# Input projection: history and edges in one piece, second weights split before the root, 1104 columns instead of 1152, odd squares...

## The reference, cut to what matters

```python
u = rmsnorm(h, norm_mix)          # h: (1088 + 16 rows, 1024)
p = u @ w_in                      # to 3336 columns
# SSD group: xbc = silu(causal_conv(p[conv columns], buf, conv_w, conv_b)), dt = softplus(p[dt] + dt_bias), z = p[gate]
# RWKV group: prev = concat([shift_buf, p[:, :-1]]); pm = p + (prev - p) * shift_mu
```

## Time and profile before

| | us |
|---|---|
| median of 3 runs | 4069.05 |
| lowest and highest | 4062.5, 4079.44 |
| span of the profiled execution | 4080.4 |

### The profile page before, as it was taken

One profiled execution on the slowest core, in us unless ns is written; L12 is line 12 of the kernel. 1 busy time (PEld: TensorE's weight loads), 2 busy tenths in 40 slices (PEclk: granted clock), 3 DMA queues, 4 the chain that ended last, 5 costly groups with the idle time before them and its releaser, 6 DMA issues.

```text
span 4080.4 us, 65406 instructions
## 1 busy us (share of the span) xinstructions
PE 3662.3 (90%) x22390; PEld 3394.8 (83%) x22390; DVE 3274.2 (80%) x6456; ACT 1167.8 (29%) x2132; POOL 1226.9 (30%) x1079
## 2 busy tenths in 40 slices
PE   7997858989897988837789999999999999999997
PEld 7997747777786755537789999999999999999996
DVE  6443666677664589999979999999999999999998
ACT  3101333223222122149932222222222222222221
POOL 1221000000000000000045555555555555655552
PEclk9998778989988998869999999999999999999998
DMA  4784330000003000004488888888888888888885
GB/s 110 88 81 67 111 101 6 21 31 12 1 9 130 23 30 24 25 31 193 198 314 297 299 288 293 296 299 288 299 299 286 297 297 289 293 299 294 290 298 185
DMA packets 289462, 723.12 MB, mean 177 GB/s; under 512 B 27336, under 2 KB 138392, under 8 KB 287808
## 3 DMA queue, kind: packets, MB, share of 16 engines
q0 software_dynamic: 119200, 426.71, 33.8%
q1 hardware_dynamic: 170144, 294.94, 21.5%
HBM read 647.26 MB, written 74.30 MB: 177 GB/s over the span
## 4 chain that ended last, share of the span: by engine, by line
PE 46%; DVE 2%; DMA 1%; issue 1%; POOL 0%; ACT 0%; DVEq 0%; POOLq 0%; ACTq 0%
PE experts_down_ps L109 8%; PE experts_down_ps L110 8%; PE experts_down_ps L111 8%; PE experts_up_ps L109 8%; PE experts_up_ps L110 8%; PE experts_up_ps L111 8%; DMA stream_u<-in_up_rows,experts_u_at 1%; DMA stream_u<-in_down,experts_v_at 0%; DVE stream_h L2990 0%; DVE stream_h_rows_of L2984 0%; DVE experts_up_lo L2947 0%; DVE experts_u_lo L2947 0%; DVE stream_h L3062 0%; DVE stream_u L2971 0%; DVE experts_act_lo L2947 0%
## 5 line engine op out<-in xcount | busy, mean ns | idle before, releaser
L2784 POOL DMA_INDIRECT stream_u<-in_up_rows,experts_u_at x384 | 540.0, 1406 | 625.4 <-DVE experts_dot L2971 509.5
L109 PE MATMUL experts_down_ps<-experts_act_hi,experts_down_hi 128*128 128x352 f32 x2048 | 676.2, 330 | 7.4 <-DVE experts_down_lo L2947 6.4
L109 PE MATMUL experts_up_ps<-experts_u_hi,experts_up_hi 128*128 128x352 f32 x2048 | 661.9, 323 | 13.0 <-DVE experts_u_lo L2947 6.6
L110 PE MATMUL experts_up_ps<-experts_u_lo,experts_up_hi 128*128 128x352 f32 x2048 | 661.3, 323 | 0.0
L111 PE MATMUL experts_up_ps<-experts_u_hi,experts_up_lo 128*128 128x352 f32 x2048 | 660.9, 323 | 0.0
L110 PE MATMUL experts_down_ps<-experts_act_lo,experts_down_hi 128*128 128x352 f32 x2048 | 660.0, 322 | 0.0
L111 PE MATMUL experts_down_ps<-experts_act_hi,experts_down_lo 128*128 128x352 f32 x2048 | 659.3, 322 | 0.0
L2791 POOL DMA_INDIRECT stream_u<-in_down,experts_v_at x384 | 515.8, 1343 | 244.0 <-issue 103.4
L2971 DVE CUSTOM_DVE_ANT_0 stream_u<-stream_u,stream_u_rows_of 128x1024 f32<-128x1024 f32 x384 | 466.5, 1215 | 78.3 <-DMA stream_u<-in_up_rows,experts_u_at 78.1
L2984 DVE SCALAR_TENSOR_TENSOR stream_h_rows_of<-stream_u,experts_weight,stream_h_rows_of 128x1024 f32<-128x1024 f32 x384 | 497.4, 1296 | 16.8 <-DVE experts_weight L2976 6.6
L2990 DVE TENSOR_TENSOR stream_h<-stream_h,experts_down_ps 128x704 f32<-128x704 f32 x512 | 450.4, 880 | 69.1 <-PE experts_down_ps L111 67.9
(11 more groups left out here) (427 smaller groups left out, 6415.2 us busy)
## 6 DMA issues: line engine op xcount, KB each, us to landing
stream_h_rest<-in_up SPq DMA_DIRECT2D x128, 512.0 KB, 4.2
stream_u<-in_down SPq DMA_DIRECT2D x128, 512.0 KB
gates<-spread_spread SPq DMA_DIRECT2D x11, 4096.0 KB, 11.5
experts_gates<-gates SPq DMA_DIRECT2D x64, 704.0 KB
cols<-inp_done POOLq DMA_DIRECT2D x26, 576.0 KB, 10.1
inp_w_in<-in_w_in SPq DMA_DIRECT2D x27, 512.0 KB, 5.8
pick_w_query<-in_w_query SPq DMA_DIRECT2D x16, 512.0 KB, 3.9
stream_u<-in_up_rows,experts_u_at POOLq DMA_INDIRECT x384
```

What stands on the lines that cost most here:

```text
L109: pe.matmul(out, w_hi, x_hi, start=start, stop=False)
L110: pe.matmul(out, w_hi, x_lo, start=False, stop=False)
L2784: pool.indirect_dma_start(u_row[b][:], None, up_rows_d, bass.IndirectOffsetOnAxis(ap=u_at[slot][:, b, a:a + 1], axis=0)).then_inc(u_row_lo ...
```

## The change

- **Columns.** The 48 columns of padding are no longer loaded, squared or projected: TI = 1104 columns in chunks of CI = 368. `raw` holds 48 fewer. The 48 columns stay in `mid`, `done` and `cols`; GpSimd zeroes them once per buffer, and `parts` and `scale_parts` split the first chunk of the dt and gate tiles around them.
- **History.** One DMA on SP's queue (2208 bytes per partition) brings the history of all tiles. GpSimd copies a tile's share into `raw` (`place_hist`, 24 columns).
- **Edges.** GpSimd copies them into a buffer (two copies, 24 and 3 columns), and one DMA stores them all at the dt tile. GpSimd no longer waits for the store of the tile before.
- **Second weights.** Those of tile 1 are rounded and split in the front, ahead of the root, not in `column_work` of tile 0.
- **Odd squares.** GpSimd makes the squares of pieces 1, 3, 5 and 7; ACT those of 0, 2, 4 and 6.

```diff
...
                 sp.dma_start(coefs[:], coef_d).then_inc(coefs_loaded, 16)
+                sp.dma_start(hist[:], hist_d).then_inc(hist_loaded, 16)
 on GpSimd
+                for k in range(1, KD, 2):
+                    pool.wait_ge(x_loaded[k], START + 16)
+                    if k >= 4:
+                        pool.wait_ge(sum_done, START + k // 2 - 1)
+                    pool.tensor_tensor(squares[:, k % 4, :], u[:, k, :], u[:, k, :], ALU.mult).then_inc(odd_square, 1)
-                def load_hist(s, m):
+                def place_hist(s, m):
                     dst = raw[s][:, 0:E_SAMPLE].rearrange("p (b w) -> p b w", b=SEQS)[:, :, 0:HIST]
-                    pool.dma_start(dst, src).then_inc(hist_loaded[s], 16)
+                    pool.tensor_copy(dst, of_tile(hist, m).rearrange("p (b w) -> p b w", b=SEQS)).then_inc(hist_placed, 1)
                 def store(q, s, m, kind):
                     if kind in ("conv", "shift"):
-                        if not (isinstance(m, int) and m == 0):
-                            pool.wait_ge(edge_stored[1 - s], (q + s) * 32)
-                            pool.wait_ge(stored[1 - s], (q + s) * 16)
                         pool.wait_ge(raw_ready, START + m + 1)
-                        load_hist(1 - s, m + 1)
-                        pool.dma_start(dst, src).then_inc(edge_stored[s], 16)
-                        pool.dma_start(at(out_p, i), raw[s][:, E_COLS - HIST:E_COLS]).then_inc(edge_stored[s], 16)
+                        place_hist(1 - s, m + 1)
+                        pool.tensor_copy(kept[:, 0:SEQS * HIST].rearrange("p (b w) -> p b w", b=SEQS), last_rows)
+                        pool.tensor_copy(kept[:, SEQS * HIST:EDGE], raw[s][:, E_COLS - HIST:E_COLS]).then_inc(edge_taken, 1)
...
-                    else:
+                    elif k % 2:
                         square(k - 1)
-                square(KD - 1)
+                act.wait_ge(w_loaded[1], START + 16)
+                act.activation(w_hi[1][:], w[1][:], ACT.Copy).then_inc(w_rounded, 1)
 ...
-                    if not (isinstance(m, int) and m == IN_TILES - 1):
+                    if not (isinstance(m, int) and m in (0, IN_TILES - 1)):
...
                 add_pair(KD - 1)
+                dve.wait_ge(w_rounded, START + 2)
+                dve.tensor_tensor(w_lo[1][:], w[1][:], w_hi[1][:], ALU.subtract).then_inc(w_split, 1)
                 dve.wait_ge(sum_done, START + KD // 2)
-                    dve.wait_ge(hist_loaded[s], q * 16 + 16)
+                    dve.wait_ge(hist_placed, START + m + 1)
                     if not first:
+                        dve.wait_ge(edge_taken, START + m - 1)
...
-                        rows, cut = slice(c * CH, c * CH + CH), slice(k * P, k * P + P)
-                        mm = product(pe, proj[s][:, c, 0:CH], w_hi[s][:, cut], w_lo[s][:, cut],
+                        rows, cut = slice(c * CI, c * CI + CI), slice(k * P, k * P + P)
+                        mm = product(pe, proj[s][:, c, 0:CI], w_hi[s][:, cut], w_lo[s][:, cut],
```

More of the change, by code:

```diff
@@ L141, in input_projection @@
         w_loaded = [sem(f"w_in_loaded_{s}") for s in range(2)]
-        hist_loaded = [sem(f"hist_loaded_{s}") for s in range(2)]
+        hist_loaded, hist_placed, edge_taken = sem("hist_loaded"), sem("hist_placed"), sem("edge_taken")
         consts_ready = sem("in_consts_ready")
-        square_ready, pair_ready = sem("square_ready"), sem("square_pair_ready")
+        square_ready, odd_square, pair_ready = sem("square_ready"), sem("odd_square_ready"), sem("square_pair_ready")
         sum_done = sem("sum_done")
@@ L154, in input_projection @@
         stored = [sem(f"in_stored_{s}") for s in range(2)]
-        edge_stored = [sem(f"edge_stored_{s}") for s in range(2)]
+        edges_stored = sem("edges_stored")
         par_loaded, dt_step, dt_act = sem("dt_par_loaded"), sem("dt_step"), sem("dt_act")
@@ L162, in tap_rest, with rest_cols, parts @@
         def tap_rest(s, j):
-            return raw[s][:, E_SAMPLE + j:E_SAMPLE + j + T - NS]
+            return raw[s][:, E_SAMPLE + j:E_SAMPLE + j + TI - NS]
+        def rest_cols(buf):
+            return buf[:, PAD1:T]
+        def parts(c):
+            lo = c * CI
+            if c == 0:
+                return (slice(0, NS), slice(0, NS)), (slice(NS, CI), slice(PAD1, PAD1 + CI - NS))
+            return ((slice(lo, lo + CI), slice(lo + PAD1 - PAD0, lo + CI + PAD1 - PAD0)),)
         CONV_OPS, SHIFT_OPS = 8, 4
@@ L212, in _ @@
             def _(pool):
-                st.start(pool, *edge_stored, *stored, *hist_loaded)
+                st.start(pool, edges_stored, *stored)
                 for s in range(2):
@@ L335, in _, with scale_parts @@
                 dve.wait_ge(coefs_loaded, START + 16)
-                dve.wait_ge(consts_ready, START + 2)
+                dve.wait_ge(consts_ready, START + 5)
                 def scale(out, src, cols):
                     return dve.tensor_tensor(out, src, inv_rms[:, cols], ALU.mult)
+                def scale_parts(out, s, c):
+                    rows = out.shape[0]
+                    for cols, to in parts(c):
+                        last = dve.tensor_tensor(out[:, to], proj[s][0:rows, c, cols.start - c * CI:cols.stop - c * CI], inv_rms[0:rows, cols], ALU.mult)
+                    return last
                 def column_work(q, s, m, kind):
-                    if not (isinstance(m, int) and m == IN_TILES - 1):
+                    if not (isinstance(m, int) and m in (0, IN_TILES - 1)):
                         dve.wait_ge(w_rounded, START + m + 2)
@@ L371, in column_work @@
                             dve.wait_ge(proj_ready, START + m * 3 + c + 1)
-                            cols = slice(c * CH, c * CH + CH)
-                            last = scale(done[s][:, cols], proj[s][:, c, 0:CH], cols)
+                            last = scale_parts(done[s][:], s, c)
                         last.then_inc(gate_ready, 1)
@@ L430, in sum_of_squares @@
                     for c in range(3):
-                        mm = pe.matmul(proj[1][:, c, 0:CH], ones[:], squares[:, k % 4, c * CH:c * CH + CH], start=(k == 1), stop=(k == KD - 1))
+                        mm = pe.matmul(proj[1][:, c, 0:CI], ones[:], squares[:, k % 4, c * CI:c * CI + CI], start=(k == 1), stop=(k == KD - 1))
                     mm.then_inc(sum_done, 1)
```

86 lines of the change are left out of this document (49 added, 37 removed).

## The result

| | before | after |
|---|---|---|
| median of the first runs, us | 4072.07 (4 runs, 4062.5 to 4079.44) | 4043.22 (4 runs, 4039.25 to 4046.23) |
| ratio, first comparison | | 0.9934 (95%: 0.9913 to 0.9956) |
| ratio, second comparison, 7 runs against 24 | | 0.9956 (0.9938 to 0.9975) |
| span of the profiled execution, us | 4080.4 | 4041.3 |

The change makes the kernel faster by 10 to 35 us by the two intervals, about 18 to 27 by their middles. The forecast was 4033, within 4018 to 4048. The profiled executions differ by 39.1 us, more than either interval has; that is what most of the experiments are about.

The account below looks back on a forecast made before the run. PE was taken to bound the first stage, with waits from a store, landing and history chain. Savings of 12.0 + 8.2 + 10.6 + 6.0 + 1.3, less 1.8 for slow starts, made 36.3 us: 4069.05 to 4033, range 4018 to 4048.

Parts of the forecast that it names:

- The bound: First stage: PE bounds it but for its waits; the loop over experts, PE-bound too, is untouched.
- the chain: Shift tiles: GpSimd waits for a store to land, then issues the history, which DVE and PE's next weights wait for.
- the three terms: First stage: PE's waits for `w_lo` 8.2 us, the dt tile's stall 10.6, half-clock starts behind stalls 6.0, all saved.
- Columns: Tiles 2 to 26: 368 columns take 166.7 ns a matmul, 6.7 less than 384, saving 12.0 us.
- Second weights: Around the root: tile 1 starts nearly 10 us earlier, but tile 2 comes 19.9 us after the sums, plus copies.
- Copies: Ahead of tile 2: GpSimd's three copies a tile lie beside DVE's work and cost 0.7 us.
- Squares: Front: four GpSimd squares of 2.7 us take turns with DVE, so the sums end 5.0 us later than by PE.
- Rival 1: Front and tiles: GpSimd beside DVE costs nothing; 42.0 us gained, 4027 us; chance 0.22.
- rival 2: Front: GpSimd's squares take longer, 4.1 us each; 30.7 us gained, 4038 us; chance 0.10.
- rival 3: Shift and dt tiles: stalls and slow starts remain in another form; 11.5 us gained, 4058 us; chance 0.03.
- rival 5: Shift and convolution tiles: GpSimd's strided copies become the bound; slower, 4136 us at 3.3 us a copy; chance 0.02.
- Rival 4: Loop over experts: moved inputs and outputs slow its transfers by 20 us; 16 us left, 4053 us; chance 0.08.

Follow-up runs that it names:

- padding_kept: The changed kernel with all 1152 columns loaded and projected; last matmul of the first stage at 372.29 us, ratio 0.9988 to the kernel before.
- odd_fills: The changed kernel with GpSimd filling the odd squares with ones instead of squaring; one run, first matmul at 10.82 us, last of the stage at 356.39.
- squares_on_act: The changed kernel with all eight squares on ACT again; last matmul of the first stage at 357.54 us, ratio 0.9962 to the kernel before.
- before_again: The kernel before, unchanged, traced a second time; last matmul of the first stage at 373.38 us, ratio 0.9997 to the kernel before.
- before_third: The kernel before, unchanged, traced a third time; last matmul of the first stage at 373.34 us, ratio 0.9992 to the kernel before.

## Why the prediction was right or wrong

**The bound** and the chain: right as a mechanism, wrong as a price. Stores, landing and history do hold the tiles, as the doubled stores show, but only by a hair: at landings of 8.5 us the chain takes 12.6 us beside PE's 12.5 and costs 1 to 2 us at most; at 10.1 to 10.8 it costs some 25. The step that failed is to take 8.2 + 10.6 + 6.0 = 24.8 us from one execution and to subtract them from the median. The page warned: the span of 4080.4 was longer than all three runs shown, and that was written off as 0.3%. (The window of 200 to 400 us, which it calls the shift tiles, holds the dt tile and gate tiles too.) For the execution that was profiled the three terms were right (measured: no wait left, 1.01 us at the dt tile, no slow starts but those behind the wait for tile 2; together 26 us). In the usual case they are 1 to 2 us together, and the sum is then 36.3 - 24.8 + 1 to 2, about 13 us. From the median of 4069.05 that would have been 4056, outside the range of 4018 to 4048.

**Columns**, 12.0 us: right in kind, too large. By 167.8 ns a step the 25 tiles save 10.0 us. The straight line through 352 and 384 columns missed by 1.1 ns. The change and padding_kept stand 10.5 to 11.5 us apart.

**Second weights:** right as a mechanism. The chain from the sums to tile 2 was given 19.9 us and 0.7 for copies; it takes 56.25 - 36.19 = 20.1 us. Tile 1 does start early and PE then waits 6.17 us for tile 2. The slow starts behind it are 11, not 12. The 1.3 us by which tile 2 was to start earlier hold the squares and copies as well; measured are 3.2 (56.25 instead of 59.46), since both of these cost less. No run has the second weights alone.

**Copies**, 0.7 us: nearly nothing ahead of tile 2. They lie beside DVE's first step of the convolution (47.44 to 48.48 us), and the third waits for its end. In the shift tiles too one copy or two wait for DVE:

```profile
...
47.46 0.21 POOL L251 COPY inp_raw<-inp_hist 128x24 f32<-128x24 f32 x1 [16.21 <-DVE inp_raw L367]
47.60 0.22 POOL L262 COPY inp_edges<-inp_raw 128x24 f32<-128x24 f32 x1
47.76 0.76 POOL L263 COPY inp_edges<-inp_raw 128x3 f32<-128x3 f32 x1
...
143.73 1.22 POOL L262 COPY inp_edges<-inp_raw 128x24 f32 x1
144.90 0.23 POOL L263 COPY inp_edges<-inp_raw 128x3 f32 x1
...
```

The forecast named a copy of over 0.9 us without a wait as a sign against it. Copies of 1.22 to 1.28 us are there, but each ends within 0.1 us of an operation of DVE, so they are copies with a wait, and three of them fit easily into PE's 12.1 us for a tile.

**Squares**, 5.0 us: right that they cost, wrong in how. A square takes 2.0 us, not 2.7, and only two of four hold DVE up. The sum of DVE's and GpSimd's busy times was not the bound; the two blocked operations stood in front of the first matmul, so the front shifts by 3.1 us as a whole, and the sums end 2.8 us later than in the first trace of before, not 4.1. The rule of the Trainium skill, "SBUF — State Buffer", section "Who interferes with whom", held in this kernel in both directions, DVE waiting for GpSimd (3.20 us for 1.36) and GpSimd for DVE (3.04 for 2.03), and in its exception for a GpSimd instruction that only writes (1.37). The factor of 1.96 of the Trainium skill's "GPSIMD Engine Reference", section 3.1, which it gives for 2048 columns, does not hold at this size: the trace has 2.02 against DVE's 1.30 for two inputs of 1104 columns, 1.55.

**The sum.** 36.3 us were forecast on the profiled execution, whose last matmul came 37.6 earlier. The terms missed both ways: columns 2 us too much, the front 2 and the waits 1 too little. On medians the gain is 29 us in the first comparison and 18 in the second. From the usual case of before the last matmul comes 11 to 13 us earlier and the next stage 10 to 12, at the edge of the second interval (10 to 25) and near the 12 to 15 at equal clock. So the 4043 us lie within the range by luck: two thirds of the sum were waits that the usual execution does not have, and the changed runs of the first comparison had a high clock. Whether one or another timed run of before had the long landings stays open, for timed runs leave no timeline.

**Rivals.** Rival 1 (no price for GpSimd beside DVE) fell by odd_fills and squares_on_act, rival 2 by the 2.0 us, rivals 3 and 5 by the list of waits. The 11.5 us of rival 3 come close to the usual gain, though for another reason: the waits were not kept, they were mostly not there before. Rival 4 named the right place for doubt, a spread of 17 us from elsewhere, and the wrong mechanism: the loop over experts lasts 2035 to 2040 us in all traces; what moves is the clock granted in the RWKV stage, 704 to 732 us.

## What to carry to other kernels

Before a wait is priced from one trace, see how far that chain's period lies above the bound beside it: a chain of DMA landings within a few per cent of PE's pace is worth nothing in one execution and 25 us in the next, and an edit that shortens PE's part moves the bound onto it. A profiled execution that lies outside the timed runs is a reason to doubt its waits. Where a part of the kernel varies with the granted clock, compare timed runs of the same clock. An operation given to an idle engine is to be priced by what it shuts out and at which moment, above all ahead of the first matmul.

## What was not expected of the hardware

- The stores of the same program took 8.4 to 8.6 us to land in three executions and 10.8 in a fourth, the weights on another queue 3.8 to 3.9 and 6.1. In the versions without the pieces of 12 bytes a store lands in 3.8 us.
- Code that was left alone, with the same matmuls, lasted 704 to 732 us, by the granted clock between 0.89 and 0.86. Which stretches have the low clock differs: in the second 40 us of the stage it is 0.64 in before_again and before_third, 0.74 in the first trace of before and 0.87 in the changed kernel. Why is not known.
- 368 columns cost 167.8 ns a step, where 384 cost 173.3 and 352, in the loop over experts, 160.0: not on a line.
- GpSimd's copies of 3 and of 24 columns both take 0.20 to 0.26 us when nothing holds them, and up to 1.28 us beside an operation of DVE.
